# A two-layer decoder step on one Trainium2 core: who reads the page numbers and issues the page loads, how a window is loaded, and where one filler projection stands

## The chip, the core and the metric

The kernel runs on one core of one Trainium2 chip. The core has a matrix engine (TensorE; PE in the profile, with PEld for its weight loads), a vector engine (VectorE, DVE), an activation engine (ScalarE, ACT), a general engine (GpSimd, POOL) and SyncE (SP), which here only issues DMAs. The engines run their own instruction streams and meet by semaphores. The metric is the time of one execution on the device, in microseconds.

## The reference

One inference step of a decoder layer, done for two layers, on 256 prompt tokens and 8 x 4 sample tokens that share all weights. Cut to what matters here:

```
z = x @ w_in                                   # conv branch and attention branch
ua, ug, q, kc, vc, ks, vs, kw, vw, gates... = split(z)
u = ua * sigmoid(ug); conv = depthwise_conv31(u); conv_out = silu(LN(conv)) @ w_conv_out
k_cmp = compress(kc_all); v_cmp = compress(vc_all)      # 32-row blocks, stride 16: (rows+pe) @ w1, gelu, @ w2
o_cmp, p_cmp = cmp_attention(q, k_cmp, v_cmp)
idx = select_blocks(p_cmp)                              # top 16 blocks of 64 rows
o_slc = slc_attention(q_rot, ks_all, vs_all, idx)
o_win = window attention (512 rows)
attn_out = (gate-weighted sum of the three) @ w_attn_out
x = LN(alpha*x + (sig(g_A)*conv_out + sig(g_B)*attn_out) @ w_o)
x = LN(alpha*x + (silu(x@w_gate) * (x@w_up)) @ w_down)
```

For the sample tokens the past of `kc, vc` (cmp) and `ks, vs` (slc) lies in pages of 128 rows in a pool; a table of 64 numbers says which page is which. The past window lies in `state_win`.

## The kernel before, in words

**Weights.** Everything is a matrix product of 128 x 128 blocks. The weights of a layer are cut into 116 chunks of 512 KB (8 blocks). SP loads chunk j into one of three slots `wch` (`load_chunk`, L482) once POOL has finished with chunk j-3. ACT writes its rounded high part `w_hi` (`high_part`, L1057; it waits until PE is through with chunk j-3), POOL the rest `w_lo` (`low_part`, L605), and PE multiplies three times: high x high, low x high, high x low (L686 to L688). So up to three chunks are split and waiting when PE asks for one, and no new one can be split until PE has used one and ACT has come round to it.

**The order of PE's work** is written out by hand. A layer begins with the outputs o = 0 to 17 of the input projection, then `compress(0)` to `compress(3)` (L782: the page batch i against `w1`), between them `second(i)` (L795), which needs the gelu of batch i from DVE (`hg_ready`). The outputs from 18 on are filler: `fill(layer)` (L729) puts one of them (24 matmuls) wherever PE would else wait. After `compress(3)` come `second(2)`, two fills (L987, L988), `second(3)`, the convolution's statistics around one more fill, and then `group_scores(0)` (L866), the scores of sample group 0. For the jobs behind it the table `FILLS` (L99) says how many fills stand in three places of each job; for job ("g", 0) these are before `group_sum(0)`, after it, and after the next job's scores. ACT and DVE walk the same numbers (`fill_out`, ACT L1217, DVE L1777): ACT reads the filler's output, then runs `high_part` three chunks on.

**Page batches.** There are 8 batches of 16 pages (128 KB a page) in each layer: 0 to 3 of the cmp cache, for `compress(0)` to `compress(3)`, 4 to 7 of the slc cache, where `group_scores(0)` reads 4 and then 5 and `group_scores(1)` 6 and 7. They share three slots `pg` (batch i in slot i mod 3, each freed by its user, `page_user`, L443). Per page SP runs a read of the number from the table into a register (`read_numbers`, L490, line L492: `TENSOR_LOAD`, a register instruction and an assertion) and a DMA that uses it (L506). SP's order: `lead` (L522) loads chunks 0 to 20 and in chunks 2 to 17 one page each of the batches 0/1 and 2; in layer 0, where batch 0 is not there yet, that makes three pages for every chunk. `body` (L545) begins with the 16 numbers of batch 3, then chunks 21 and 22, the 16 numbers of batch 4, chunk 23, and then the DMAs of batch 3, the DMAs of batch 4, the numbers of batch 5 and its DMAs; chunk 24 comes behind them. All of this is one stream on SP, and every transfer of SP is on one queue.

**Windows.** `load_window` (L509) loads the 2 MB of one sample group as four DMAs of 512 KB: four in a row in layer 0's `lead`, and otherwise one behind every chunk or every other chunk. The state of the convolution (`load_past`, 544 KB) follows eight chunks after the next layer's first window DMA.

Of the kernel before, what the change touches and what calls it, by code (L numbers as in the profile page):

```python
# [68 lines left out]
EARLY = 18  # L69
FIRST_GU = CH_IN + CH_MIX + CH_WO  # L70
LEAD = EARLY + PAIRS
PG_SLOTS = 3

# [25 lines left out]
FILLS = {("g", 0): (1, 2, 1), ("u", 0): (0, 1, 1), ("u", 1): (0, 0, 1), ("u", 2): (0, 1, 1), ("u", 3): (0, 0, 0), ("g", 1): (1, 1, 1),  # L99
# [52 lines left out]
def decoder_kernel(nc, xT, consts, page_table, weights, small, w1, w2, cmp_pages, slc_pages, win, past_u,  # L152
                   yT, kv_out, p_conv_out, s_conv_out, win_out):
    with ExitStack() as ctx:  # L154
# [148 lines left out]
        win_in = Signal("win_in", 2, 16 * DEC_B // 2, ahead=False)  # L303
# [105 lines left out]
        carrier_pe = ctx.enter_context(nc.semaphore("carrier_pe"))  # L409
        carrier_sp = ctx.enter_context(nc.semaphore("carrier_sp"))  # L410
# [58 lines left out]
        def _(sp):  # L469
# [20 lines left out]
            def read_numbers(i, first=0, n=2 * PAGES):  # L490

                return [sp.value_load(table[0:1, bass.ds((i % 4) * 2 * PAGES + j, 1)], min_val=0, max_val=POOL - 1)  # L492
                        for j in range(first, first + n)]

            def load_pages(layer, i, first=0, n=2 * PAGES, numbers=None):

                slot = i % PG_SLOTS
                source = cmp_pages if i < 4 else slc_pages
                if numbers is None:
                    numbers = read_numbers(i, first, n)  # L500
                if first == 0:
                    user, back = before(i, 8, PG_SLOTS)
                    sig, count = page_user(user)
                    wait_alone(*sig(layer, count - back * sig.per_layer))
                for j, page in zip(range(first, first + n), numbers):
                    sp.dma_start(pg[:, slot, bass.ds(j, 1)], source[bass.ds(layer, 1), bass.ds(page, 1)].rearrange(  # L506
                        "a b p n -> p (a b) n")).then_inc(pages_in[slot].sem, 16)

            def load_window(layer, gr, rows=range(DEC_B // 2)):  # L509
                if rows[0] == 0:  # L510
                    wait_alone(*gpv_done(layer, gr))
                    wait_alone(*win_stored(layer, gr))
                for b in rows:
                    sp.dma_start(wn[:, b:b + 1], win[bass.ds(layer, 1), 4 * gr + b:4 * gr + b + 1].rearrange(
                        "a b p n -> p (a b) n")).then_inc(win_in.sem, 16)
# [6 lines left out]
            def lead(layer, first):  # L522


                for j in range(LEAD):
# [9 lines left out]
                    if EARLY - 2 * PAGES <= j < EARLY:  # L535
# [5 lines left out]
                        load_pages(layer, 2, n, 1)  # L541
# [3 lines left out]
            def body(layer, more):  # L545


                numbers = {3: read_numbers(3)}
                for j in range(LEAD, CHUNKS):
                    load_chunk(layer, j)  # L550

                    if j == EARLY + AHEAD - 2:
                        numbers[4] = read_numbers(4)
                    if j == EARLY + AHEAD - 1:
                        load_pages(layer, 3, numbers=numbers[3])
                        load_pages(layer, 4, numbers=numbers[4])
                        load_pages(layer, 5)
# [3 lines left out]
                    n = j - (EARLY + AHEAD + 5)  # L561
                    if 0 <= n < 4:
                        load_window(layer, 1, [n])
# [6 lines left out]
                    if more and 0 <= n - 2 * PAGES < 8 and n % 2 == 0:  # L570
                        load_window(layer + 1, 0, [(n - 2 * PAGES) // 2])
                    if more and n == 2 * PAGES + 8:
                        load_past(layer + 1)
# [84 lines left out]
        def _(pe):  # L658
# [271 lines left out]
            with layers(pe) as layer:  # L930
# [57 lines left out]
                fill(layer)  # L988
# [58 lines left out]
        def _(act):  # L1047
# [161 lines left out]

            for n in range(PAIRS):  # L1210
                high_part(0, n)
            hi_ready.count = 0
            with layers(act) as layer:
# [13 lines left out]
                def chunk_read(o):  # L1227

                    high_part(layer, o + PAIRS)
# [751 lines left out]
```

## Time and profile before

| | us |
|---|---|
| median of 3 runs (1072.98 to 1074.56) | 1073.44 |
| the profiled execution's own time | 1073.44 |
| its span in the trace | 1071.6 |
| PE busy | 1001.3 (93%) |
| POOL busy | 753.0 (70%) |
| DVE busy | 606.7 (57%) |
| ACT busy | 524.2 (49%) |
| mean share of the 16 DMA engines in SP's queue | 49.5% |

The span is from the first to the last recorded instruction. Busy time of an engine is the union of its instructions; register, semaphore and DMA-issuing instructions are not counted in it. A layer takes about half of the span: layer 0 is at `group_scores(0)` at 138.5 us, layer 1 at 662.7 us. In lists of waits, "idle" is the time in which the engine had nothing running just before an instruction, with the instruction or DMA that ended last before it.

### The profile page before, as it was taken

The page shows a single profiled execution, that of the slowest core. Times are in us where ns is not written, and L with a number is a line of the kernel's source. Part 1 is how long each engine was busy: PE and PEld are TensorE (multiplying, and loading weights), DVE is VectorE, ACT ScalarE, POOL GpSimd, SP SyncE. Part 2 cuts the span into 40 slices and gives each one's busy share as a digit, 9 for nine tenths or more (in the row PEclk, how much of TensorE's full clock was granted, in tenths as well). Part 3 has the DMA queues.
Part 4 walks back from the last instruction along what each step waited for, and adds up shares of the span by engine and source line. Part 5 has one row for each costly group of instructions (what it writes and reads, how often), then busy time and mean ns, then how long its engine had stood idle before and what let it go on. Part 6 is the DMA issues. An engine that isn't in the chain of part 4 may idle for free.

```text
span 1071.6 us, 23755 instructions
## 1 busy us (share of the span) xinstructions
PE 1001.3 (93%) x7646; PEld 945.2 (88%) x7646; DVE 606.7 (57%) x1386; ACT 524.2 (49%) x966; POOL 753.0 (70%) x1081
## 2 busy tenths in 40 slices
PE   4999989988999999999979999898989999999995
PEld 4998878787999999999979977787879899999995
DVE  1868765556777555511446794745575775554124
ACT  3352563454565555544354335643455566555335
POOL 5778744344778888898757785543349788889984
PEclk9999999999999999999999999999999999999998
DMA  8775687421356764555367456664115345545542
GB/s 307 226 245 200 194 275 239 173 80 60 109 166 191 225 217 160 172 172 166 100 218 230 155 178 201 237 211 157 61 60 168 128 158 161 172 160 164 174 152 87
DMA packets 78342, 185.11 MB, mean 173 GB/s; under 512 B 9474, under 2 KB 42626, under 8 KB 77698
## 3 DMA queue, kind: packets, MB, share of 16 engines
q1 hardware_dynamic: 74322, 171.22, 49.5%
q10 hardware_dynamic: 3744, 11.40, 2.8%
q8 instruction: 64, 1.05, 0.4%
q0 software_dynamic: 144, 0.89, 0.2%
q14 instruction: 68, 0.56, 0.2%
HBM read 170.90 MB, written 12.57 MB: 171 GB/s over the span
## 4 chain that ended last, share of the span: by engine, by line
POOL 67%; issue 31%; POOLq 1%; DMA 1%; ACT 0%; SPq 0%
POOL w_lo L614 61%; POOL hid L637 3%; POOL res L635 2%; POOL res L644 1%; DMA wch<-weights_in 0%; POOLq L608 0%; DMA table<-page_table_in 0%; POOLq L632 0%; POOLq L154 0%; ACT w_hi L1064 0%; POOL hid L638 0%; POOL hid L635 0%; SPq L472 0%; POOLq L620 0%; POOLq L624 0%
## 5 line engine op out<-in xcount | busy, mean ns | idle before, releaser
L614 POOL TENSOR_TENSOR w_lo<-wch,w_hi 128x256 fp32r<-128x256 f32 x940 | 685.6, 766 | 307.2 <-ACT w_hi L1064 306.8
L686 PE MATMUL proj<-x_hi,w_hi 128*128 128x290 f32 (+1 forms) x1248 | 379.5, 304 | 25.4 <-POOL w_lo L614 20.6
L687 PE MATMUL proj<-x_hi,w_lo 128*128 128x290 f32 (+1 forms) x1248 | 370.4, 297 | 0.0
L688 PE MATMUL proj<-x_lo,w_hi 128*128 128x290 f32 (+1 forms) x1248 | 369.8, 296 | 0.0
L1064 ACT ACTIVATE w_hi<-wch 128x1024 fp32r<-128x1024 f32 x235 | 247.6, 1054 | 159.2 <-PE proj L709 75.7
L686 PEld LDWEIGHTS proj<-x_hi,w_hi 128*128 128x128 f32 x1248 | 235.6, 189 | 32.3 <-issue 21.5
L687 PEld LDWEIGHTS proj<-x_hi,w_lo 128*128 128x128 f32 x1248 | 236.5, 190 | 0.5
L688 PEld LDWEIGHTS proj<-x_lo,w_hi 128*128 128x128 f32 x1248 | 236.3, 189 | 0.0
L707 PE MATMUL proj<-hid_hi,w_hi 128*128 128x288 f32 x352 | 104.3, 296 | 0.0
L709 PE MATMUL proj<-hid_lo,w_hi 128*128 128x288 f32 x352 | 103.6, 294 | 0.0
L708 PE MATMUL proj<-hid_hi,w_lo 128*128 128x288 f32 x352 | 103.3, 293 | 0.0
L1436 DVE SCALAR_TENSOR_TENSOR ps_s<-u_p,sm,ps_s 128x256 f32<-128x256 f32 x232 | 94.5, 483 | 4.2
L1520 DVE SCALAR_TENSOR_TENSOR res<-proj,res 128x288 f32<-128x288 f32 x32 | 14.6, 456 | 130.9 <-PE proj L709 109.6
L1069 ACT ACTIVATE res<-res,top 128x256 f32<-128x256 f32 (+5 forms) x108 | 46.7, 433 | 52.9 <-DVE top L1597 48.5
L1850 DVE COPY sums_of<-proj 128x2 f32<-128x2 f32 x88 | 14.0, 160 | 99.9 <-PE proj L688 99.7
L708 PEld LDWEIGHTS proj<-hid_hi,w_lo 128*128 128x128 f32 x352 | 66.2, 188 | 0.1
L707 PEld LDWEIGHTS proj<-hid_hi,w_hi 128*128 128x128 f32 x352 | 66.1, 188 | 0.1
L709 PEld LDWEIGHTS proj<-hid_lo,w_hi 128*128 128x128 f32 x352 | 66.1, 188 | 0.0
L1069 ACT ACTIVATE q_raw<-q_raw,sums_of 128x288 f32<-128x288 f32 x44 | 23.6, 538 | 76.0 <-DVE q_raw L1863 76.0
L686 PE MATMUL proj<-mix_hi,w_hi 128*128 128x288 f32 x128 | 38.6, 302 | 0.5 <-POOL w_lo L614 0.5
L770 PE MATMUL ps_t<-cst 128*128 128x128 f32 x324 | 38.7, 277 | 0.0
L770 PEld LDWEIGHTS ps_t<-cst 128*128 128x128 f32 x324 | 37.4, 192 | 1.2 <-issue 1.0
(287 smaller groups left out, 1568.4 us busy)
## 6 DMA issues: line engine op xcount, KB each, us to landing
wch<-weights_in SPq DMA_DIRECT2D x235, 512.0 KB, 3.7
pg<-cmp_pages_in SPq DMA_DIRECT2D x128, 128.0 KB, 2.9
pg<-slc_pages_in SPq DMA_DIRECT2D x128, 128.0 KB, 2.5
wn<-win_in SPq DMA_DIRECT2D x16, 512.0 KB, 5.4
win_out<-wn ACTq DMA_DIRECT2D x4, 2048.0 KB, 8.5
hid<-w_in SPq DMA_DIRECT2D x2, 1024.0 KB, 5.5
kv_out<-kv ACTq DMA_DIRECT2D x2, 864.0 KB, 3.9
res<-xT_in SPq DMA_DIRECT2D x1, 1152.0 KB, 5.4
```

What stands on the lines that cost most here:

```text
L614: last = nc.gpsimd.tensor_tensor(lo[:, cols], raw[:, cols], hi[:, cols].bitcast(F32), ALU.subtract)
L637: do(nc.gpsimd.tensor_tensor(out, out, tap_s[:], ALU.add))
L686: mm(ps, hi[:, kb], x[0][:, kb, 0:n], start=kb == 0, stop=False)
L687: mm(ps, lo[:, kb], x[0][:, kb, 0:n], start=False, stop=False)
L688: last = mm(ps, hi[:, kb], x[1][:, kb, 0:n], start=False, stop=kb == KD - 1)
L707: mm(ps, hi, hid_hi[:, kb], start=kb == 0, stop=False)
L708: mm(ps, lo, hid_hi[:, kb], start=False, stop=False)
L709: last = mm(ps, hi, hid_lo[:, kb], start=False, stop=kb == KF - 1)
L770: mm(ps_m[:, 0:P], k("mean_c"), k("cos")[:, 0:P], start=True, stop=True)
L1064: hi_ready.up(nc.scalar.activation(w_hi[:, n % PAIRS].rearrange("p k n -> p (k n)"), wch[:, n % SLOTS].rearrange("p k n -> p (k n)"), ACT. ...
L1069: i = nc.scalar.activation(out, in_, func, **kw)
L1436: i = v.scalar_tensor_tensor(out=out, in0=in_, scalar=conv_w[:, c, tap:tap + 1], in1=so_far, op0=ALU.mult, op1=ALU.add)
```

## The change

Four things are changed.

1. SP's page numbers: `read_numbers` is gone. `load_pages` reads the up to 16 numbers of a batch itself, directly before that batch's DMAs (for a whole batch: the reads, then the wait for the slot, then the DMAs). So the numbers of batches 3 and 4 are now read behind chunk 23.
2. Page batch 2 is no longer issued by SP. A new function `load_page` on ACT reads one number and issues one page's DMA behind the `high_part` of outputs 2 to 17.
3. Windows: one DMA of 2 MB for a group instead of four of 512 KB; `load_past` for the next layer now directly follows the window's DMA, where the first of the four stood.
4. One fill is taken from before `second(3)` (on PE, ACT and DVE), and the first number of `FILLS["g", 0]` goes from 1 to 2.

```diff
-FILLS = {("g", 0): (1, 2, 1), ...
+FILLS = {("g", 0): (2, 2, 1), ...
-        win_in = Signal("win_in", 2, 16 * DEC_B // 2, ahead=False)
+        win_in = Signal("win_in", 2, 16, ahead=False)
...
-            def load_pages(layer, i, first=0, n=2 * PAGES, numbers=None):
+            def load_pages(layer, i, first=0, n=2 * PAGES):
...
+                for at in range(first, first + n, READ_AHEAD):
+                    some = range(at, min(at + READ_AHEAD, first + n))
+                    pages = [sp.value_load(table[0:1, bass.ds((i % 4) * 2 * PAGES + j, 1)], min_val=0, max_val=POOL - 1) for j in some]
+                    if at == 0:
+                        user, back = before(i, 8, PG_SLOTS)
+                        sig, count = page_user(user)
+                        wait_alone(*sig(layer, count - back * sig.per_layer))
+                    for j, page in zip(some, pages):
+                        sp.dma_start(pg[:, slot, bass.ds(j, 1)], source[bass.ds(layer, 1), bass.ds(page, 1)].rearrange(
+                            "a b p n -> p (a b) n")).then_inc(pages_in[slot].sem, 16)
+
+            def load_window(layer, gr):
+                wait_alone(*gpv_done(layer, gr))
+                wait_alone(*win_stored(layer, gr))
+                win_in.up(sp.dma_start(wn[:], win[bass.ds(layer, 1), 4 * gr:4 * gr + 4].rearrange("a b p n -> p (a b) n")))
...
-                        load_pages(layer, 2, n, 1)
...
-                numbers = {3: read_numbers(3)}
                 for j in range(LEAD, CHUNKS):
                     load_chunk(layer, j)
-                    if j == EARLY + AHEAD - 2:
-                        numbers[4] = read_numbers(4)
                     if j == EARLY + AHEAD - 1:
-                        load_pages(layer, 3, numbers=numbers[3])
-                        load_pages(layer, 4, numbers=numbers[4])
-                        load_pages(layer, 5)
+                        for i in range(3, 6):
+                            load_pages(layer, i)
...
-                    n = j - (EARLY + AHEAD + 5)
-                    if 0 <= n < 4:
-                        load_window(layer, 1, [n])
+                    if j == EARLY + AHEAD + 5:
+                        load_window(layer, 1)
...
-                    if more and 0 <= n - 2 * PAGES < 8 and n % 2 == 0:
-                        load_window(layer + 1, 0, [(n - 2 * PAGES) // 2])
-                    if more and n == 2 * PAGES + 8:
+                    if more and n == 2 * PAGES:
+                        load_window(layer + 1, 0)
                         load_past(layer + 1)
...
                 second(layer, 2)
                 fill(layer)
-                fill(layer)
                 second(layer, 3)
...
+            def load_page(layer, i, j):
...
+                page = act.value_load(table[0:1, bass.ds((i % 4) * 2 * PAGES + j, 1)], min_val=0, max_val=POOL - 1)
+                act.dma_start(pg[:, slot, bass.ds(j, 1)], cmp_pages[bass.ds(layer, 1), bass.ds(page, 1)].rearrange(
+                    "a b p n -> p (a b) n")).then_inc(pages_in[slot].sem, 16)
...
                 def chunk_read(o):
                     high_part(layer, o + PAIRS)
+                    if EARLY - 2 * PAGES <= o:
+                        load_page(layer, 2, o - (EARLY - 2 * PAGES))
```

How the change moves instructions on SP, behind chunk 20 and layer 0's window, in the kernel before (the left number is the source line; 16 reads or 16 DMAs stand where the dots are):

```order
L514 DMA wn<-win_in 128x1024 x4
L576 UNCONDITIONAL_BRANCH
L492 TENSOR_LOAD table
...
L487 DMA wch<-weights_in 128x1024 x2
L492 TENSOR_LOAD table
...
L487 DMA wch<-weights_in 128x1024
L506 ISA
L506 DMA pg<-cmp_pages_in 128x256
...
L506 DMA pg<-slc_pages_in 128x256
```

The same place in the changed kernel:

```order
L510 DMA wn<-win_in 128x4x1024
L564 UNCONDITIONAL_BRANCH
L489 DMA wch<-weights_in 128x1024 x3
L498 TENSOR_LOAD table
...
L504 DMA pg<-cmp_pages_in 128x256
L498 TENSOR_LOAD table
...
L504 DMA pg<-slc_pages_in 128x256
```

Chunks 21 to 23 stand in front, and behind them the 16 reads of batch 3, its 16 DMAs, the 16 reads of batch 4, its DMAs, the 16 reads of batch 5 and its DMAs; before, the reads of batches 3 and 4 stood ahead of chunks 21 and 23.

On ACT, from the end of `second_out(2)` (the two `v_misc` rows) through the fills to `second_out(3)` (the `k_cmp` row), before:

```order
L1069 ACTIVATE v_misc<-ps_o 31x256
L1076 REGISTER_ALU
L1077 ACTIVATE hid<-proj 128x288
L1060 REGISTER_ALU
L1064 ACTIVATE w_hi<-wch 128x1024
L1076 REGISTER_ALU
L1077 ACTIVATE hid<-proj 128x288
L1064 ACTIVATE w_hi<-wch 128x1024
L1069 ACTIVATE k_cmp<-ps_o 128x128
```

The same place in the changed kernel:

```order
L1056 ACTIVATE v_misc<-ps_o 31x256
L1063 REGISTER_ALU
L1064 ACTIVATE hid<-proj 128x288
L1047 REGISTER_ALU
L1051 ACTIVATE w_hi<-wch 128x1024
L1056 ACTIVATE k_cmp<-ps_o 128x128
```

One filler's output (`hid<-proj`) and one chunk's high part (`w_hi`) are gone from here; PE's 24 matmuls of that filler are gone from the same place. They stand again behind the first window store:

```order
L1295 DMA win_out<-wn 128x4x1024
L1063 REGISTER_ALU
L1064 ACTIVATE hid<-proj 128x288
L1047 REGISTER_ALU
L1051 ACTIVATE w_hi<-wch 128x1024
L1063 REGISTER_ALU
L1064 ACTIVATE hid<-proj 128x288
L1047 REGISTER_ALU
L1051 ACTIVATE w_hi<-wch 128x1024
L1056 ACTIVATE res,hid<-res,top 128x1056
```

Before, there was one such pair between the store and the exponential of the 1056 columns.

On ACT again, between the high parts made for outputs 2 and 3 (`chunk_read`), the first page load in the changed kernel:

```order
L1051 ACTIVATE w_hi<-wch 128x1024
L1203 ISA
L1205 TENSOR_LOAD table
L1205 ISA x2
L1206 ISA
L1206 DMA pg<-cmp_pages_in 128x256
L1047 REGISTER_ALU
L1050 REGISTER_ALU
L1051 ACTIVATE w_hi<-wch 128x1024
```

Before, the two `w_hi` rows followed each other with only register instructions between them.

## Rows read from the trace of the kernel before

**Rows 1.** PE's waits, whole span: us in total, times, longest us.
```profile
PE proj L686 <- POOL w_lo L614: 21.2, 9, 15.0
PE ps_t L848 <- DVE imp L1613: 8.3, 10, 1.3
```

**Rows 2.** PE's timeline around `second(3)` of layer 0: start us, us, what.
```profile
122.26 0.40 PE L686 MATMUL proj<-x_hi,w_hi 128*128 128x288 f32 x1
...
128.62 0.29 PE L688 MATMUL proj<-x_lo,w_hi 128*128 128x288 f32 x1
129.04 0.43 PE L810 MATMUL ps_o<-res,w_sb 64*64 64x128 f32 x4
```

**Rows 3.** DVE's timeline there: the gelu of batch 3, last step, both layers.
```profile
128.21 0.68 DVE L1487 SCALAR_TENSOR_TENSOR res<-sq 64x512 f32<-64x512 f32 x1
...
652.40 0.68 DVE L1487 SCALAR_TENSOR_TENSOR res<-sq 64x512 f32<-64x512 f32 x1
```

**Rows 4.** PE's timeline, layer 1: `second(3)`, and the wait at `group_sum(0)`.
```profile
653.23 0.44 PE L810 MATMUL ps_o<-res,w_sb 64*64 64x128 f32 x4
...
671.11 0.39 PE L897 MATMUL ps_t<-imp,cst 128*128 128x14 f32 x2 [0.52 <-DVE imp L1641]
```

**Rows 5.** SP's number reads (L492) of batch 3, layer 0: ns min/median/max, first and last start.
```profile
L492 SPq TENSOR_LOAD <-table x16: 261/261/275, 81.8 to 90.0; - x16
```

**Rows 6.** SP's timeline, both layers: chunks 21 to 23, then the DMAs of batch 3.
```profile
90.54 9.88 SPq L487 DMA_DIRECT2D wch<-weights_in  x3
100.69 8.49 SPq L506 DMA_DIRECT2D pg<-cmp_pages_in  x16
...
621.06 9.23 SPq L506 DMA_DIRECT2D pg<-cmp_pages_in  x16
```

**Rows 7.** SP's DMAs (L506) of batch 5 with their landing: layer 0, then layer 1.
```profile
L506 SPq DMA_DIRECT2D pg<-slc_pages_in x16: 332/333/668, 127.4 to 136.2; - x16
DMA to landing us min/median/max: 2.1/2.5/5.6
...
L506 SPq DMA_DIRECT2D pg<-slc_pages_in x16: 332/333/487, 649.5 to 657.5; - x16
DMA to landing us min/median/max: 1.9/2.2/6.8
```

**Rows 8.** POOL's timeline: the low part of chunk 20, layer 0 and layer 1.
```profile
88.22 3.01 POOL L614 TENSOR_TENSOR w_lo<-wch,w_hi 128x256 fp32r<-128x256 f32 x4 [1.68 <-ACT w_hi L1064]
...
612.48 3.01 POOL L614 TENSOR_TENSOR w_lo<-wch,w_hi 128x256 fp32r<-128x256 f32 x4 [2.44 <-ACT w_hi L1064]
```

**Rows 9.** PEld's timeline: `group_scores(0)` comes to batch 5, layer 0 and layer 1.
```profile
140.96 0.15 PEld L885 LDWEIGHTS ps_s<-pg,qs_rot 128*32 128x32 f32 x4 [0.67 <-DMA pg<-slc_pages_in]
...
664.38 0.19 PEld L885 LDWEIGHTS ps_s<-pg,qs_rot 128*32 128x32 f32 x6 [0.31 <-issue]
```

**Rows 10.** PE's timeline: `compress(3)` begins, layer 0 and layer 1.
```profile
114.40 6.90 PE L792 MATMUL ps_w<-pg,hid 128*128 128x256 f32 x31
...
638.65 6.68 PE L792 MATMUL ps_w<-pg,hid 128*128 128x256 f32 x30
```

**Rows 11.** PE's timeline at the start of the kernel.
```profile
14.97 0.60 PE L686 MATMUL proj<-x_hi,w_hi 128*128 128x288 f32 x1 [14.97 <-POOL w_lo L614]
...
18.25 0.66 PE L691 MATMUL ps_t<-x_hi,w_hi 128*128 128x288 f32 x2
18.73 0.32 PE L686 MATMUL proj<-x_hi,w_hi 128*128 128x288 f32 x1
...
19.16 0.43 PE L691 MATMUL ps_t<-x_hi,w_hi 128*128 128x288 f32 x2
```

**Rows 12.** Busy us (count) of PE, PEld, DVE, ACT, POOL, PEclk, DMA share, GB/s.
```profile
28.00:64.00 36.00, 36.00 (x272) 35.00 (x270) 24.02 (x61) 13.78 (x21) 26.65 (x38) 1.00 0.74 231
138.00:144.00 6.00, 5.52 (x38) 2.15 (x39) 4.68 (x12) 0.60 (x2) 1.46 (x3) 1.00 0.95 292
265.00:270.00 5.00, 4.04 (x25) 3.48 (x26) 1.92 (x5) 1.19 (x3) 2.78 (x4) 0.79 0.21 57
1060.00:1064.00 4.00, 0.04 (x1) 0.00 (x0) 3.13 (x7) 3.65 (x9) 0.00 (x0) 0.90 0.00 0
```

**Rows 13.** SP's timeline in layer 0's lead: three pages and a chunk.
```profile
36.73 1.94 SPq L506 DMA_DIRECT2D pg<-cmp_pages_in  x3
38.72 0.43 SPq L487 DMA_DIRECT2D wch<-weights_in  x1
```

**Rows 14.** PE's waits from 28 to 80 us, then from 535 to 560 us.
```profile
PE ps_w L778 <- POOL w_lo L614: 0.7, 1, 0.7
PE proj L686 <- POOL w_lo L614: 0.5, 1, 0.5
...
PE proj L686 <- DVE u_s L1701: 2.2, 1, 2.2
PE proj L686 <- POOL w_lo L614: 2.1, 2, 1.4
```

**Rows 15.** ACT waiting for a weight chunk beside the window loads, 350 to 400 us.
```profile
ACT w_hi L1064 <- DMA wch<-weights_in: 3.5, 8, 1.1
```

More of the change, by code:

```diff
@@ L72 @@
 PG_SLOTS = 3
+READ_AHEAD = 16
 SMALL = {}
@@ L96 @@
 JOBS = [("g", 0)] + [("u", n) for n in range(4)] + [("g", 1)] + [("u", n) for n in range(4, 8)]
-FILLS = {("g", 0): (1, 2, 1), ("u", 0): (0, 1, 1), ("u", 1): (0, 0, 1), ("u", 2): (0, 1, 1), ("u", 3): (0, 0, 0), ("g", 1): (1, 1, 1),
+FILLS = {("g", 0): (2, 2, 1), ("u", 0): (0, 1, 1), ("u", 1): (0, 0, 1), ("u", 2): (0, 1, 1), ("u", 3): (0, 0, 0), ("g", 1): (1, 1, 1),
          ("u", 4): (0, 1, 2), ("u", 5): (0, 0, 2), ("u", 6): (0, 2, 1), ("u", 7): (0, 1, 0)}
@@ L409, in decoder_kernel @@
         carrier_pe = ctx.enter_context(nc.semaphore("carrier_pe"))
+        carrier_act = ctx.enter_context(nc.semaphore("carrier_act"))
         carrier_sp = ctx.enter_context(nc.semaphore("carrier_sp"))
@@ L488, in load_chunk @@
                     "a p (k n) -> p (a k) n", k=8)))
-            def read_numbers(i, first=0, n=2 * PAGES):
-                return [sp.value_load(table[0:1, bass.ds((i % 4) * 2 * PAGES + j, 1)], min_val=0, max_val=POOL - 1)
-                        for j in range(first, first + n)]
-            def load_pages(layer, i, first=0, n=2 * PAGES, numbers=None):
+            def load_pages(layer, i, first=0, n=2 * PAGES):
                 slot = i % PG_SLOTS
                 source = cmp_pages if i < 4 else slc_pages
[L499 to L515, printed above, removed]
+                for at in range(first, first + n, READ_AHEAD):
[8 more added lines that the diff above has]
+                            "a b p n -> p (a b) n")).then_inc(pages_in[slot].sem, 16)
@@ L1207, in group_act @@
                     do(sq[:, 0:1024], ps_s[:].rearrange("p a n -> p (a n)"), ACT.Copy, gpt_act)
+            def load_page(layer, i, j):
+                slot = i % PG_SLOTS
+                if j == 0:
+                    user, back = before(i, 8, PG_SLOTS)
+                    sig, count = page_user(user)
+                    act.wait_ge(*sig(layer, count - back * sig.per_layer))
+                    act.sem_inc(carrier_act, 1)
+                page = act.value_load(table[0:1, bass.ds((i % 4) * 2 * PAGES + j, 1)], min_val=0, max_val=POOL - 1)
+                act.dma_start(pg[:, slot, bass.ds(j, 1)], cmp_pages[bass.ds(layer, 1), bass.ds(page, 1)].rearrange(
+                    "a b p n -> p (a b) n")).then_inc(pages_in[slot].sem, 16)
             for n in range(PAIRS):
@@ L1212, in _ @@
             hi_ready.count = 0
+            act.wait_ge(table_in, 16)
             with layers(act) as layer:
@@ L1275, in _ @@
                 second_out(layer, 2)
-                fill_out()
                 fill_out()
```

1 line of the change is left out of this document (removed).

## The prediction

> **What bounds the kernel now.** I read the engines' busy shares first: PE is busy for 1001.3 of 1071.6 us. The list of PE's waits comes next [rows 1]: the largest group is 21.2 us for POOL's low parts, of which 15.0 are the start of the kernel, and the next is 8.3 us in ten small gaps. So PE's instruction stream is the clock of this kernel: whatever puts a hole into it lengthens the span by that hole, and taking work off another engine gives back at most a gap that PE has now. Then I went along PE's timeline and looked, at each place that the change touches, at what comes just in time. Two things do: the gelu for `second(3)`, and page batch 5 for `group_scores(0)`. The change moves both edges the wrong way.
>
> The sum is made against the profiled execution: 1071.6 us of span and 1.8 us around it, 1073.44 us, which is also the median.
>
> **The moved fill.** Two fills stand between `second(2)` and `second(3)`. They start at 122.26 and the last matmul starts at 128.62, that is 3.3 us for a fill, and `second(3)` starts at 129.04 [rows 2]. DVE finishes the gelu it needs at 128.21 + 0.68 = 128.89 [rows 3]. That chain starts with `compress(3)` and runs on DVE and ACT; no fill is in it. With one fill less PE is there at about 125.7 and still starts `second(3)` at 129.04: a hole of 3.3 us, and the 24 matmuls are done later. Layer 1 is the same (gelu at 653.08, `second(3)` at 653.23) [rows 3, 4]. What the fill can cover in its new place is the gap before `group_sum(0)`, 0.5 us in layer 1 and none in layer 0 [rows 4]. Cost: 3.3 + 2.8 = 6.1 us. Bounds: 0 if the gelu came 3.3 us earlier, which nothing in the change does, and about 5 a layer if chunk 23, whose high part moves behind the window store on ACT, also came late. I take it as covered by the next wait.
>
> **The page numbers.** The 16 reads of a batch start from 81.8 to 90.0 and the next DMA is at 90.54 [rows 5, 6]: 8.7 us of SP for 16 numbers, 0.54 each. Before, 16 reads were done while SP had nothing to issue (chunk 21 had to wait anyway), and 16 more ahead of chunk 23. Now SP takes chunk 23 as soon as POOL has finished chunk 20, at 88.22 + 3.01 = 91.2 in layer 0 [rows 8]. Then: chunk 23 until 91.7, the reads of batch 3 until 100.4, its first DMA at 100.7. That is where it was (100.69) [rows 6]. But between the DMAs of batches 3 and 4 there are now 16 reads, so batches 4 and 5 and chunk 24 go 8.7 us later. The last DMA of batch 5 goes from 136.2 to 144.9, and with the median landing of 2.5 us it is in at 147.4 [rows 7]. PE takes batch 5 at 140.96, after a wait of 0.67 us for just this DMA [rows 9]; in the changed kernel it arrives at the same time (the hole above is before it) and waits until 147.4: +6.4 us. In layer 1 SP ran ahead before: batch 3 started at 621.06. Now chunk 23 waits for POOL until 615.5 [rows 8], batch 3 starts at 616.0 + 8.7 + 0.3 = 625.0, 3.9 us later; with the second group of reads, batch 5's last DMA goes from 657.5 to 670.1 and lands at 672.3, where PE wants it at 664.5 [rows 7, 9]: +7.8 us. Batch 3 stays in time: its last DMA goes at about 109 and 634, and `compress(3)` starts at 114.40 and 638.65 [rows 6, 10]. Bounds for one layer: 0, if these reads overlap DMA issue in some way that the single stream of SP does not show, and 9.5 at the slowest landing seen, 5.6 [rows 7]. That one fell beside the store of the convolution's state, which will be over by then, so I take the median.
>
> The Trainium skill, "DMA: Bandwidth & Descriptors", section "Latency and other measured facts", gives a floor of about 600 ns for such a register load. By it 16 reads would take an estimated 9.6 us, and each page term would be 0.9 us larger. This trace has 0.26 us for the load alone and 0.54 for one number with all that goes with it, and the sum goes by that.
>
> Chunk 24 is issued 8 to 9 us later as well. Its high part is made behind the window store, after 150 us, so it has time.
>
> **TensorE's clock.** PE will now stand still for about 6.5 us before batch 5. The rows show what that does: at the end the last matmul is over at 1060.04, and in 1060 to 1064 the granted clock is 0.90 [rows 12], so it falls to the lower level (1.2 GHz) at about 1063.2, 3.2 us after the last work. At the start a pair of matmuls takes 0.66 us until 18.73 and 0.43 after [rows 11]: 3.8 us at half speed, 1.9 us lost. I charge 1.9 us for each of the two long waits, 3.8 us. The wait of 3.3 us before `second(3)` may cost the same, but what it slows ends before batch 5 is there. Bounds: 0, and 3.8 a layer if two falls count.
>
> **Batch 2 on ACT.** In layer 0's lead SP takes 1.94 us for the DMAs of three pages, 0.43 for the chunk [rows 13] and 1.3 for the reads left out of that row, 3.7 us for a chunk that PE uses up in 3.2. SP is never idle there, while the DMA engines are busy for 0.74 [rows 12]. Afterwards PE has waits of 0.7 and 0.5 us for low parts [rows 14]. With a third of the pages gone SP keeps up: -1.2 us. The Trainium skill, "DMA: Bandwidth & Descriptors", section "Issuing engines are not separate DMA queues", says that issuing on several engines saves only the sequencer's time. If that saving were small here, as it says is usual, this term would be nothing; the rows say that the sequencer is what is short. In layer 1 PE waits 2.2 us for DVE, which waits for the small weights' DMA, and then up to 1.4 for a low part whose chunk was late [rows 14]. Before these DMAs SP has one page less to issue, 1.1 us, and then another: -1.6 us. Bounds for both: 0 and -4.7. ACT pays 1.1 us for a page. It works for less than 14 us of the 36 from 28 to 64 [rows 12], and the last page is issued before DVE takes up the compressed rows, so I put nothing on it; if it were all exposed it would be 1 us a layer.
>
> **Windows.** The merged window with the convolution's state is 2.5 MB ahead of a chunk, at the 292 GB/s that the rows show [rows 12] 9 us, so the chunk lands some 4 us later than now. ACT already waits for chunks there, 3.5 us in eight waits [rows 15], while PE has no gap, since three chunks are split ahead of it. I take 0; bounds 0 and +4, once.
>
> **Sum.** 6.1 + 6.4 + 7.8 + 3.8 - 1.2 - 1.6 = +21.3 us, which gives 1094.7. I say 1094.
>
> **The rivals.**
> - *The numbers cost less than their 8.7 us on the path.* If batch 5 were in time, what is left is the fill less the lead's gain, +6.1 - 2.8 = +3.3: 1076.7. For it: SP ran 4 us ahead in layer 1. Against it: in layer 0 PE waits for this very DMA already [rows 9]. A half-way case, +4 a layer without the clock, gives 1085.
> - *Everything adds.* Chunk 23 late by 2 us a layer, the clock twice in each layer, the window's burst: +21.3 + 4 + 3.8 + 2 = 1104.
> - *About no change.* Batch 5 in time and the hole before `second(3)` filled by half: 1074 to 1075.
> - *Faster.* The mechanism is the lead: SP is relieved by a third, both starts of the layers lose their gaps, at most 1.2 + 3.5 us, and the fill ends in a place that needs it. That is 1069 to 1071. It decides only if batch 5 lands before 141 and 664.5 us and the gelu is there by 125.7; I find no row for either.
>
> **How the numbers follow.** The full mechanism 0.62 (own range 1088 to 1101), numbers cheaper 0.17, everything adds 0.10, no change 0.07, faster 0.04. The range 1081 to 1102 holds the first case, about half of the second and some of the third. A measurement tells about 0.2%, 2.1 us, from no change; so faster 0.04, same 0.07, slower 0.89.
>
> **What would show it.** A wait of PE at the batch-5 scores for the page DMA, 6 to 8 us in each layer; a wait of about 3.3 us before `second(3)` for DVE's gelu; granted clock under 1 in the microseconds behind the batch-5 wait; SP's DMAs of batch 5 ending near 145 and 670; the two small waits near 68 and 76 us gone. The prediction is wrong if PE's wait at batch 5 is under 3 us, or if `compress(3)` waits for batch 3.

## The result, and the profile after

| | before | after |
|---|---|---|
| median | 1074.00 us (1072.98 to 1074.79, 4 runs) | 1106.86 us (1102.54 to 1110.21, 4 runs) |
| span of the profiled run | 1071.6 us | 1105.7 us |
| mean granted clock | 0.994 | 0.977 |

The ratio is 1.0304, with a 95% interval from 1.0262 to 1.0348: the changed kernel is 28 to 37 us slower. The prediction was 1094, range 1081 to 1102. The direction was right, the size was not: 21.3 us of extra span were forecast, and the profiled run has 34.1. One execution of the kernel `r_busy` below fell into a slow state (1261.9 us at a granted clock of 0.755) and is not in its ratio.

The list of PE's waits in the changed kernel (us in total, times, longest us) answers to [rows 1]:

```profile
PE proj L674 <- POOL w_lo L602: 24.3, 8, 14.9
PE ps_s L873 <- DMA pg<-slc_pages_in: 13.5, 2, 7.4
PE ps_o L798 <- DVE res L1488: 8.4, 4, 3.3
PE ps_t L836 <- DVE imp L1614: 7.7, 10, 1.3
```

Two groups are new: 13.5 us for the pages of batch 5, and 8.4 us for the gelu, which was 1.9 before. The low parts' group has grown by 3.1. The next lines are PE's timeline at these places, both layers (start us, us, what, idle time before and what ended it); they answer to [rows 2, 4, 9]:

```profile
127.54 0.44 PE L798 MATMUL ps_o<-res,w_sb 64*64 64x128 f32 x4 [3.28 <-DVE res L1488]
148.84 1.07 PE L873 MATMUL ps_s<-pg,qs_rot 128*32 128x512 f32 x2 [7.45 <-DMA pg<-slc_pages_in]
389.50 0.61 PE L674 MATMUL proj<-x_hi,w_hi 128*128 128x290 f32 x1 [3.22 <-POOL w_lo L602]
672.64 0.69 PE L798 MATMUL ps_o<-res,w_sb 64*64 64x128 f32 x4 [3.27 <-DVE res L1488]
```

The two holes of 3.3 us before `second(3)` are where the prediction put them, and so is the page wait. The hole at 389.50, in the FFN of layer 0, was not predicted. SP's DMAs of batch 5 in both layers, with their landing, answer to [rows 7]:

```profile
L504 SPq DMA_DIRECT2D pg<-slc_pages_in x16: 332/333/345, 136.8 to 144.6; - x16
...
DMA to landing us min/median/max: 2.1/2.4/4.2
```

```profile
L504 SPq DMA_DIRECT2D pg<-slc_pages_in x16: 332/333/333, 681.6 to 689.5; - x16
...
DMA to landing us min/median/max: 2.0/2.3/4.1
```

The last issue at 144.6 was predicted as 144.9. But PE starts at 148.84, which is 4.2 us behind it: the slowest landing, not the median. Layer 1 is the same, 689.5 + 4.1 = 693.6, and PE's weight load is at 693.68. The windows over these places (columns as in [rows 12]) show the clock:

```profile
128.00:132.00 4.00, 4.00 (x16) 2.97 (x15) 1.00 (x11) 1.49 (x4) 3.01 (x4) 0.62 0.34 104
...
144.00:148.00 4.00, 0.00 (x0) 0.00 (x0) 1.31 (x7) 1.72 (x3) 0.00 (x0) 0.75 0.79 242
148.00:152.00 4.00, 3.16 (x12) 0.87 (x14) 0.00 (x0) 0.00 (x0) 0.00 (x0) 0.50 0.81 234
...
388.00:392.00 4.00, 2.50 (x10) 2.50 (x11) 2.12 (x5) 3.00 (x5) 4.00 (x7) 0.54 0.38 116
392.00:396.00 4.00, 4.00 (x21) 4.00 (x20) 0.42 (x2) 0.00 (x0) 2.95 (x5) 0.60 0.45 149
```

Behind each of these holes the granted clock falls, so that windows of 4 us show 0.50 to 0.62: TensorE is at its lower level (1.2 GHz) for some microseconds, behind the short holes too.

The lag of an instruction is how much later it starts than the same instruction in the trace of before. Its growth gives the bill by stages. "Measured" is the growth in the stage, "predicted" are the prediction's own terms:

| stage | lag at its end | measured | predicted |
|---|---|---|---|
| layer 0 up to its FFN | +13.7 | 13.7 | 10.4 (6.4 page, 3.3 fill, 1.9 clock, -1.2 lead) |
| layer 0's FFN and output | +19.5 | 5.8 | 0 |
| layer 1's lead | +19.4 | -0.1 | -1.6 |
| rest of layer 1 | +34.1 | 14.7 | 12.5 (7.8 page, 2.8 fill, 1.9 clock) |

### The profile page after: what moved, and what is told of

It is laid out like the page before. It is cut to its first block, busy times and chain, and to the rows that moved or that the text cites. A ratio compares the mean times of both kernels' runs of the same rounds, so it can differ in the third digit from the quotient of the medians.

```text
span 1105.7 us, 23747 instructions
## 1 busy us (share of the span) xinstructions
PE 1017.0 (92%) x7646; PEld 955.9 (86%) x7646; DVE 604.8 (55%) x1386; ACT 523.7 (47%) x966; POOL 749.3 (68%) x1081
## 4 chain that ended last, share of the span: by engine, by line
POOL 65%; issue 33%; POOLq 1%; DMA 1%; ACT 0%; SPq 0%
POOL w_lo L602 59%; POOL hid L625 3%; POOL res L623 2%; POOL res L632 0%; DMA wch<-weights_in 0%; DMA table<-page_table_in 0%; POOLq L596 0%; POOLq L620 0%; POOLq L155 0%; ACT w_hi L1051 0%; POOL hid L626 0%; POOL hid L623 0%; SPq L474 0%; POOLq L608 0%; POOLq L612 0%
```

## The experiments

All are compared with the kernel before, run beside them on the same chip; a cost in us is the ratio less 1, times 1074.

### The four parts, each alone

**Windows and state** (`w_only`): only part 3 of the change.

```diff
-                    if more and 0 <= n - 2 * PAGES < 8 and n % 2 == 0:
-                        load_window(layer + 1, 0, [(n - 2 * PAGES) // 2])
-                    if more and n == 2 * PAGES + 8:
+                    if more and n == 2 * PAGES:
+                        load_window(layer + 1, 0)
                         load_past(layer + 1)
```

> The kernel before with one part of the change: each window is one transfer of 2 MB, and the convolution's state follows it directly. Theory (the burst holds up the weight chunk behind it): in the changed kernel the chunk behind the 2.5 MB lands 9.1 us after its issue, PE waits 3.2 us for a low part in layer 0's FFN and then runs some 5 us at half clock, 5.8 us later in all. Alone it should cost about the same: +4 to +6.5 us, a PE wait of about 3 us near 375 us into the span. Rival (the prediction's own term: three split chunks cover the late one, and the loss in the changed kernel came from its other parts): within +-1 us, and no PE wait over 1 us there.

Measured: ratio 1.0077 (1.0060 to 1.0093), +8.3 us. The theory's place and its PE wait were right, its size a bit low; the prediction's zero is refuted. The chunk behind the window is issued at 363.27, ACT gets it at 372.58, and PE then stands still:

```profile
372.58 1.06 ACT L1059 ACTIVATE w_hi<-wch 128x1024 fp32r<-128x1024 f32 x1 [5.79 <-DMA wch<-weights_in]
```

```profile
376.55 0.61 PE L681 MATMUL proj<-x_hi,w_hi 128*128 128x290 f32 x1 [3.29 <-POOL w_lo L609]
```

**Reads** (`r_only`): only part 1.

```diff
-                numbers = {3: read_numbers(3)}
...
-                    if j == EARLY + AHEAD - 2:
-                        numbers[4] = read_numbers(4)
...
-                        load_pages(layer, 3, numbers=numbers[3])
-                        load_pages(layer, 4, numbers=numbers[4])
+                        load_pages(layer, 3)
+                        load_pages(layer, 4)
```

> The kernel before with one part of the change: the page numbers of batches 3 and 4 are read behind chunk 23, directly before their DMAs. Theory (SP's reads set batch 5's arrival, the slowest landing counts, and TensorE's clock falls behind each long wait): PE waits of 7 to 8 us in layer 0 and 6 to 8 us in layer 1 before the batch-5 scores, 1.7 to 2.5 us of slow clock behind each: +17 to +20 us. Rival 1 (the reads cost as predicted with the median landing): +14.2 and 3.8 of clock, about +18, but then the holes are 6.4 and 7.8. Rival 2 (in the changed kernel the page wait is made by the batch-2 pages or the window on the queue, and the reads are cheap): under +5 us.

Measured: ratio 1.0198 (1.0181 to 1.0215), +21.3 us. The waits, each PE's first matmul on batch 5:

```profile
148.65 1.07 PE L882 MATMUL ps_s<-pg,qs_rot 128*32 128x512 f32 x2 [8.77 <-DMA pg<-slc_pages_in]
...
682.62 1.07 PE L882 MATMUL ps_s<-pg,qs_rot 128*32 128x512 f32 x2 [8.59 <-DMA pg<-slc_pages_in]
```

The reads alone make the page waits; batch 2 on ACT, the window and the fill are not needed for them. Both holes are 0.6 to 0.8 us longer than the theory had.

**Fill** (`f_only`): only part 4.

```diff
-FILLS = {("g", 0): (1, 2, 1), ...
+FILLS = {("g", 0): (2, 2, 1), ...
...
                 fill(layer)
-                fill(layer)
                 second(layer, 3)
```

> The kernel before with one part of the change: one fill moves from before second(3) to before group_sum(0). Theory (each layer gets a hole of 3.3 us, and the clock falls behind it too): 2 x 3.3 us of holes and 1.7 to 2.8 us of slow clock behind each, less the 0.7 us wait for batch 5 in layer 0 and the 0.5 us gap at group_sum(0) in layer 1: +9 to +11 us, a granted clock under 1 in the 8 us behind the holes. Rival (the prediction's term: the hole alone): +5.5 to +6.1 us and no fall of the clock. Second rival (the fill covers something in its new place): under +3 us.

Measured: ratio 1.0124 (1.0108 to 1.0141), +13.3 us, more than either theory. PE's timeline shows what both had left out:

```profile
153.44 0.40 PE L686 MATMUL proj<-x_hi,w_hi 128*128 128x288 f32 x1 [2.17 <-ACT hid L1076]
...
158.32 0.40 PE L686 MATMUL proj<-x_hi,w_hi 128*128 128x288 f32 x1 [1.41 <-POOL w_lo L614]
```

In its new place the fill finds two more fills behind it, whose output buffers and weight chunks depend on ACT, and ACT is behind the window store: 3.6 us a layer, in place of some 1 us of shorter waits that the kernel before has here. In the changed kernel neither wait exists at this place (PE's timeline has no wait for `hid` there), because batch 5 comes so late that ACT is done. It was a bound of the prediction ("about 5 a layer if chunk 23 ... also came late. I take it as covered by the next wait"), and it was covered.

**Batch 2 on ACT** (`a_only`): only part 2.

> The kernel before with one part of the change: batch 2's 16 page numbers are read and its DMAs issued by ACT instead of SP. Theory from the two traces: the lead of layer 0 loses its gaps near 68 and 76 us (-1.2 to -1.5 us), layer 1's start gains nothing, because the small weights and the low part behind them stay late: -1.0 to -1.6 us. Rival (the prediction's term): -2.8 us, half of it in layer 1. Second rival (ACT pays the 1.1 us a page on the path): 0 to +2 us.

Measured: ratio 0.9998 (0.9988 to 1.0008), -0.2 us, with 10 runs. The -2.8 us of the prediction are refuted, and the theory's -1.0 to -1.6 isn't reached either. In the trace, which is of the fastest of the ten, the first layer's `compress(0)` is 1.3 us earlier and layer 1's start adds 0.5; in the changed kernel's trace it adds 0.1.

### What the window's burst is made of

**Window merged, state late** (`w_late_past`):

```diff
                     if more and n == 2 * PAGES:
                         load_window(layer + 1, 0)
+                    if more and n == 2 * PAGES + 8:
                         load_past(layer + 1)
```

> The kernel before with each window as one transfer of 2 MB, but the convolution's state left eight chunks behind it, as before. With the state directly behind the window it was 7.7 us slower, the chunk behind landed after 9.2 us, and PE waited 3.3 us and then lost 2.5 at half clock. Theory (bytes ahead of the chunk decide: 0.54 MB less at some 290 GB/s is 1.9 us earlier): the chunk lands after some 7.3 us, PE waits about 1.4 us near 375 us, the clock stays up or nearly, +1 to +3.5 us. Rival (the merge alone does it, whatever the state does): +6 to +8 us.

Measured: ratio 1.0032 (1.0020 to 1.0045), +3.4 us, within the theory's range, though landing and wait are each 0.9 us longer than it had. The chunk behind lands after 8.2 us (its group's slowest), and PE waits:

```profile
374.48 0.40 PE L682 MATMUL proj<-x_hi,w_hi 128*128 128x290 f32 x1 [2.29 <-POOL w_lo L610]
```

```profile
376.00:380.00 4.00, 4.00 (x32) 4.00 (x31) 1.58 (x4) 0.75 (x2) 4.00 (x6) 1.00 0.67 232
```

The clock stays at 1.00 behind this hole of 2.3 us, where in `w_only` it was 0.50 in 376 to 380 behind one of 3.3. So the state costs one further microsecond of hole, and in these traces the clock with it.

These kernels give the rule that the prediction lacked. Chunk j is issued when POOL frees its slot; PE then still has three chunks of 3.2 us to work on, some 10 us in the changed kernel (376.30 to 386.3). In that time the chunk must land, ACT must take 1.06 us and POOL 3.01. So a landing of up to about 5.9 us is free, and every further microsecond is PE's hole: 9.1 gives 3.2 (measured 3.22), 9.2 gives 3.3 (3.29), 8.2 gives 2.3 (2.29), and in `wa` below 9.3 gives 3.4 (3.41). Before, the slowest chunk there landed in 5.6 us: the four pieces left 0.3 us of margin.

```profile
L487 SPq DMA_DIRECT2D wch<-weights_in x10: 327/328/328, 358.9 to 388.4; - x10
...
DMA to landing us min/median/max: 3.6/4.3/5.6
```

### What the reads cost, and the clock behind the wait

**Only batch 4's numbers late** (`r4_only`); those of batch 3 stay where they are:

```diff
-                    if j == EARLY + AHEAD - 2:
-                        numbers[4] = read_numbers(4)
...
-                        load_pages(layer, 4, numbers=numbers[4])
+                        load_pages(layer, 4)
```

> The kernel before with only the numbers of batch 4 read late (between the DMAs of batch 3 and 4); those of batch 3 stay ahead of chunk 21. Moving both groups cost 20.8 us. Theory (SP stands free from about 81 us until POOL is done with chunk 20 at 91; that slack holds one group of 16 reads, so only the second group that leaves the front lands on the path): within +-1.5 us of before, DMAs of batch 5 ending at 136 to 137 and before 661 us. Rival (each group costs its half): +8 to +12 us.

Measured: ratio 1.0059 (1.0042 to 1.0076), +6.3 us. Both expectations missed: one group is neither free nor half of the 21.3. SP's timeline:

```profile
89.36 1.28 SPq L487 DMA_DIRECT2D wch<-weights_in  x3
93.44 8.56 SPq L506 DMA_DIRECT2D pg<-cmp_pages_in  x16
111.41 27.73 SPq L506 DMA_DIRECT2D pg<-slc_pages_in  x32
```

Chunk 23 is out at about 90.6, but the DMAs of batch 3 start only at 93.44, 7.3 us earlier than before [rows 6] and not 8.7: between them SP issues nothing for 2.8 us. (Their slot is freed by `compress(0)`, which has just ended then; that this is the cause is read from the code and was not tried.) Batch 4 starts 2.0 us later than before, the last DMA of batch 5 about 2.6 later, and PE waits 3.24 us in layer 0 and 3.03 in layer 1. There were some 7 us of free time on SP for these reads, and the first group overdraws them by 2. The second group doesn't add all of its 8.7. These are SP's DMAs of batches 4 and 5 in `r_only` and before:

```profile
116.70 27.99 SPq L506 DMA_DIRECT2D pg<-slc_pages_in  x32
```

```profile
109.42 27.10 SPq L506 DMA_DIRECT2D pg<-slc_pages_in  x32
```

They end at 144.7 in `r_only`, 139.1 in `r4_only` and 136.5 before. So in layer 0 the second group adds 5.6 us: that fits 8.7 less the 2.8 us in which SP stood still here.

**Extra matmuls in the page wait** (`r_busy`, `r_busy2`). Both are `r_only` with a number of matmuls of 128 columns in front of batch 5, whose results are overwritten by the next fill; 34 in the first, 46 in the second:

```diff
                 for b in range(4):
+                    if gr == 0 and b == 2:
+                        hold_clock(layer, 46)
                     if b % 2 == 0:
```

> The kernel with only the reads moved (20.8 us slower than before) and 34 extra matmuls of 128 columns, whose results nobody reads, in the two waits of 8.8 and 8.6 us before the batch-5 scores. Theory: the waits themselves are 8.8 - 0.7 + 8.6 = 16.7 us and the clock behind them is the rest, about 4: +15.5 to +17.5 us, clock 1.00 behind the wait. Rival (the rest is not the clock but late chunks behind the reads): +20 to +21 us as without them.

> The kernel with only the reads moved (21.3 us slower than before) and 46 extra matmuls of 128 columns, whose results nobody reads, in the page wait of 8.8 us, so that no idle time is left in it. Theory (1.5 to 2.5 us a layer of the cost is slow clock behind the wait): clock 1.00 behind it and, with up to 1 us a layer by which the extra matmuls run over, +17 to +19.5 us. Rival (the clock behind the wait costs nothing on the path): +21 to +23 us.

Measured: 1.0177 (1.0139 to 1.0214) and 1.0183 (1.0165 to 1.0202), +19.0 and +19.7 us. Neither is told apart from the 1.0198 of `r_only`, and neither decides between its theory and its rival. With 34 there was still a hole of 1.9 us, and the clock fell behind it; in layer 1 the hole was 1.7 us and the clock stayed at 1.00. These are windows of `r_busy` in layer 0:

```profile
148.00:152.00 4.00, 2.07 (x20) 1.68 (x22) 0.00 (x0) 0.00 (x0) 0.00 (x0) 0.99 0.70 236
152.00:156.00 4.00, 4.00 (x17) 0.81 (x9) 0.00 (x0) 0.00 (x0) 0.00 (x0) 0.58 0.82 235
```

With 46 it stayed up in both layers (windows of `r_busy2`, then of `r_only`):

```profile
148.00:152.00 4.00, 3.98 (x37) 3.59 (x40) 0.00 (x0) 0.00 (x0) 0.00 (x0) 1.00 0.76 229
```

```profile
144.00:148.00 4.00, 0.00 (x0) 0.00 (x0) 1.30 (x7) 0.23 (x2) 0.00 (x0) 0.58 0.79 233
148.00:152.00 4.00, 3.35 (x14) 0.97 (x16) 0.00 (x0) 0.00 (x0) 0.00 (x0) 0.56 0.80 232
```

The extra matmuls ran over, so that the first scores of batch 5 came 2.8 us later than in `r_only` (3.4 in layer 1), of which 1.1 (1.6) were there before the page wait. But the next common point was only 1.4 us later (282.56 against 281.10), and 1.1 in layer 1 (811.26 against 810.14). What they gave back is 1.4 and 2.3 us. That is one trace of each kernel, and it agrees with the prediction's 1.9 for each page wait; by the times alone it stays open.

### The clock behind the hole of 3.3 us

**Extra matmuls before `second(3)`** (`f_busy`): `f_only` with 13 of them behind the one fill.

> The kernel before with the fill moved (13.8 us slower alone) and 13 extra matmuls of 128 columns before second(3), whose results nobody reads, in the hole of 3.3 us. Theory (the hole is 3.3, the fill's late output costs 2.2 + 1.4 in its new place, and 1 to 2 us a layer are the clock behind the hole): clock 1.00 in 128 to 136 us and +9.5 to +12 us. Rival (the clock fall is hidden under what follows, as the prediction had it): +13 to +14 us as without them.

Measured: ratio 1.0067 (1.0050 to 1.0084), +7.2 us, against +13.3 without them, and the intervals don't touch. The gelu still sets the start of `second(3)`; the only difference is that PE isn't idle ahead of it. The windows, `f_only` first:

```profile
128.00:132.00 4.00, 3.31 (x16) 2.80 (x17) 2.10 (x17) 2.65 (x6) 2.19 (x3) 0.50 0.59 162
132.00:136.00 4.00, 4.00 (x18) 3.29 (x18) 1.42 (x2) 0.84 (x2) 0.80 (x2) 0.68 0.98 247
```

```profile
128.00:132.00 4.00, 3.60 (x33) 3.21 (x33) 3.56 (x21) 3.62 (x9) 0.59 (x1) 1.00 0.33 97
132.00:136.00 4.00, 4.00 (x28) 3.74 (x27) 1.42 (x2) 1.64 (x3) 2.44 (x4) 1.00 0.98 253
```

So a hole of 3.3 us costs about as much again, 3 us a layer, behind it. That was more than the theory's 1 to 2. The traces have less in layer 1: between the hole and the window store the lag against `f_only` shrinks by 2.8 us in layer 0 and by 1.7 in layer 1. There the clock falls later, behind the wait of 2.16 us for the fill's late output (`f_busy`):

```profile
684.00:688.00 4.00, 4.00 (x21) 3.86 (x20) 3.53 (x7) 3.57 (x6) 4.00 (x5) 0.62 0.93 370
```

**The changed kernel with both** (`after_busy`): 13 before `second(3)` and 26 before batch 5.

> The changed kernel with 13 extra matmuls of 128 columns before second(3) and 26 before the batch-5 scores, whose results nobody reads, in the time in which TensorE stands still (3.3 and 6 to 7.5 us): the waits stay as long, only the engine isn't idle in them. Theory (a part of the loss is TensorE at its lower clock behind the holes, some 8 to 10 us in all, more than the 3.8 of the prediction): 7 to 10 us faster than the changed kernel, +23 to +26 us against before, clock near 1 behind both holes. Rival (the prediction's 3.8 us): +28 to +30 us. Second rival (the extra matmuls delay more than they hold): +33 or more.

Measured: ratio 1.0265 (1.0237 to 1.0294), +28.5 us: the rival's 28 to 30 and not the theory's 23 to 26. It is 4.2 below the changed kernel's 32.7, but with overlapping intervals. PE still waits for the pages, and it waits for them up to about the same time as without the extra matmuls:

```profile
149.39 1.07 PE L881 MATMUL ps_s<-pg,qs_rot 128*32 128x512 f32 x2 [4.65 <-DMA pg<-slc_pages_in]
```

It was 148.84 in the changed kernel and is 149.39 here. The first hole's clock costs up to 3 us where nothing waits behind it, but here it is hidden by the page wait, as the prediction had it.

### Do the parts add up?

Alone they cost 8.3, 21.3, 13.3 and -0.2, in sum 42.7; together 32.7. Seven kernels look for the 10 us: the changed kernel without one part, and pairs on top of before.

> The changed kernel with the page numbers read as before (batch 3 ahead of chunk 21, batch 4 ahead of chunk 23): windows, fill and batch 2 on ACT stay changed. The parts alone cost 7.7 (windows), 20.8 (reads), 13.8 (fill) and -0.3 us (batch 2 on ACT), 42 in sum, while together they cost 33. Theory (the fill's late output on ACT and POOL, 3.6 us a layer, lies under the wait for batch 5, so reads and fill overlap and nothing else does): the parts without the reads add up, +19 to +22 us, so the reads are worth only 11 to 14 in the changed kernel. Rival (windows and the others overlap instead): under +15 us.

> The changed kernel with the fill back before second(3): windows, reads and batch 2 on ACT stay changed. Theory (overlap of fill and reads): windows 7.7 + reads 20.8 - 0.3 = +27 to +29 us, so the moved fill is worth only 4 to 6 us here against 13.8 alone. Rival (the overlap is elsewhere): 33 - 13.8 = +18 to +20 us.

> The changed kernel with the windows in four pieces and the convolution's state late, as before: reads, fill and batch 2 on ACT stay changed. Theory (the windows are independent of the rest): 33 - 6 to 7.7 = +25 to +27 us, no PE wait near 390 us. Rival (without the burst something else is late there, since the fill and reads overlap accounts for all of the 9 us that the parts exceed the whole): +29 or more.

> The kernel before with the reads and the fill moved, and nothing else. Alone they cost 21.3 and 13.3 us. Theory (the fill's late output on ACT and POOL, 2.2 + 1.4 us a layer, lies under the wait for batch 5, and half of the clock's fall behind the first hole too): +26 to +29 us. Rival (they add up): +33 to +36 us.

> The kernel before with the windows merged and the reads moved. Alone they cost 8.3 and 21.3 us. Theory (different places, no overlap): +28 to +31 us. Rival (the merged window changes what SP has to do ahead of the reads and takes back part of the loss, as the changed kernel without the moved fill, +21.4 us, suggested): +20 to +24 us.

> The kernel before with the windows merged and the fill moved. Alone they cost 8.3 and 13.3 us. Theory (no overlap): +20 to +23 us. Rival (as the changed kernel with the reads as before, +13.5 us, suggested): +13 to +16 us.

> The kernel before with the windows merged and batch 2 on ACT. Alone they cost 8.3 and -0.2 us. Theory (batch 2 on ACT gains only where something else has made SP late, and with merged windows it does: 5 to 7 us): +1.5 to +4 us. Rival (the two add up and the rest is scatter between chips): +7 to +9 us.

| kernel | parts | ratio (95%) | us | sum of its parts |
|---|---|---|---|---|
| `rf` | reads, fill | 1.0265 (1.0247 to 1.0284) | 28.5 | 34.6 |
| `wr` | windows, reads | 1.0265 (1.0242 to 1.0287) | 28.5 | 29.6 |
| `wf` | windows, fill | 1.0183 (1.0162 to 1.0204) | 19.7 | 21.6 |
| `wa` | windows, ACT | 1.0036 (1.0023 to 1.0049) | 3.9 | 8.1 |
| `no_window` | reads, fill, ACT | 1.0252 (1.0221 to 1.0282) | 27.1 | 34.4 |
| `no_reads` | windows, fill, ACT | 1.0126 (1.0090 to 1.0162) | 13.5 | 21.4 |
| `no_fill` | windows, reads, ACT | 1.0199 (1.0170 to 1.0227) | 21.4 | 29.4 |
| changed kernel | all | 1.0304 (1.0262 to 1.0348) | 32.7 | 42.7 |

The theories of `rf`, `wr`, `wa` and, within the interval, `no_window` and `wf` were met; those of `no_reads` and `no_fill` were missed by 5.5 us or more, towards their rivals. Reads and fill overlap by about 6 us. Under the page wait lie both the fill's late output (no wait for `hid` or a low part is left there in the trace of `rf`) and the slow clock behind the first hole; how the 6 us split between the two was not measured. Windows add up with either within the intervals. The rest lies with batch 2 on ACT, which is worth nothing alone and about 4 us beside merged windows (`wa` against `w_only`; their intervals don't touch), more in `no_reads` and `no_fill` with wider intervals. I don't know why. In the trace of `wa` PE still waits 3.41 us near 374 us and the clock falls behind it, so the burst itself isn't mended. The traces don't show the gain: with batch 2 on ACT the span of the profiled execution is 1.2 us shorter in `wa` than in `w_only`, 0.2 shorter in `no_reads` than in `wf`, and 0.4 longer in `no_fill` than in `wr`. These pairs ran on different chips, each beside its own kernel before, so a difference between chips isn't excluded. This part stays open.

### A version that beats both

**Batch 2 on ACT, and layer 1's small weights a chunk earlier** (`a_small`):

```diff
-                    if j == SLOTS:
+                    if j == (SLOTS if first else SLOTS - 1):
                         small_in.up(sp.dma_start(w1_sb, ...
```

> A version meant to beat both kernels: the kernel before with batch 2 on ACT, and in layer 1 the two small weights of compress issued one chunk earlier (behind chunk 2 instead of chunk 3), since DVE waits 9.5 us for them there and PE 2.2 us for DVE. If PE's wait at 559 us is set by them: 1 to 2 us faster than before. Rival (the weight chunks behind come later by their bytes and PE waits for a low part instead): no difference, within +-1 us.

Measured: ratio 0.9954 (0.9936 to 0.9973), median 1070.57 us beside 1073.64: 3 to 7 us faster than before, where the theory had 1 to 2. In the trace of before PE waits here three times: for a low part, for DVE, which waited 9.5 us for these weights, and for a low part again. In the new one the first wait has grown, the second has shrunk and the third is gone (before, then `a_small`):

```profile
546.86 0.41 PE L686 MATMUL proj<-x_hi,w_hi 128*128 128x288 f32 x1 [0.66 <-POOL w_lo L614]
...
552.57 0.40 PE L686 MATMUL proj<-x_hi,w_hi 128*128 128x288 f32 x1 [2.24 <-DVE u_s L1701]
...
557.43 0.40 PE L686 MATMUL proj<-x_hi,w_hi 128*128 128x288 f32 x1 [1.39 <-POOL w_lo L614]
```

```profile
547.45 0.40 PE L686 MATMUL proj<-x_hi,w_hi 128*128 128x288 f32 x1 [1.51 <-ACT sig_u L1077]
...
552.37 0.40 PE L686 MATMUL proj<-x_hi,w_hi 128*128 128x288 f32 x1 [1.45 <-POOL w_lo L614]
```

The two lines of `a_small` are at the places of the first two lines of before (62 and 86 matmuls behind the layer's first). Together the waits shrink by 1.3 us, from 4.3 to 3.0, and the spans differ by 2.3. The times say more than the trace explains. Nor was the small weights' move tried alone: against `a_only` (-0.2 us) the intervals don't touch, but the trace of `a_only` has the third wait gone too, and there the second is 1.90.

## Why the prediction was off

- **The failed step is the windows.** "ACT already waits for chunks there ... while PE has no gap, since three chunks are split ahead of it. I take 0; bounds 0 and +4, once." It predicted the late chunk well (some 4 us later; 9.1 against 5.6 at most before). It didn't subtract that from a cover: 10 us, less 4.1 of ACT and POOL, leave 5.9 for the landing. The hole is 3.2 us. With the clock behind it the stage costs 5.8 in the trace of the changed kernel and 6.0 in that of `w_only`, whose times say 8.3. This one term is nearly half of the miss of 12.8 us of span, and it is outside its own bound of +4. With 5.8 in its place the sum would be 1100.5.
- **The page wait: right mechanism, short by 1.5 to 2 us a layer.** SP's times were met within 0.3 us (144.6 for 144.9) in layer 0; in layer 1 the last issue, 689.5 less the lag of 19.4, is the 670.1 of the prediction. The median landing was the wrong row: PE needs all 16 pages, and the last came after 4.2 and 4.1 us. The upper bound in the prediction used the slowest one. (The rest of layer 1's excess is within this.) One reading behind it was wrong and did no harm: chunk 21 did not "have to wait anyway". SP issues it at 90.54 before, and at 81.11 in `r_only`, where the reads aren't in front of it.
- **The hole before `second(3)`: right, 3.28 and 3.27 for 3.3.** That its clock would be hidden under the page wait was right as well (`after_busy`), and so was that the fill's late output would be.
- **The clock behind the page waits: 1.9 each was about right** (1.4 and 2.3 from the traces of `r_busy2`), but two falls were left out. One is behind the burst's hole. The other is near 280 us, where the granted clock is 0.50 in 280 to 284 and the changed kernel loses 1.3 us against the one before, whose own fall, near 270, is shorter.
- **The lead: -2.8 was wrong, -0.2 measured alone.** In layer 0 the gaps near 68 and 76 us did go, and the lag shrinks by 1.9 us there in the changed kernel's trace; in layer 1 only 0.1 came. The times of `a_only` (-1.3 to +0.9 us) hardly show it, and why stays open.
- **Of the rivals,** "everything adds" (1104, chance 0.10) is nearest to 1106.9. It had the clock twice and the window at 2 us, but chunk 23 late by 2 us a layer, which did not happen in the changed kernel. "Numbers cheaper", "no change" and "faster" are refuted by the waits above.

## What to carry over

When a step puts more bytes ahead of something on the same queue, don't ask whether a buffer is "ahead": write down the time from its issue to its use, take off every engine that must still touch it, and compare what is left with the slowest landing (here 10.0 - 1.06 - 3.01 = 5.9 us, of which 5.6 were used before). Waits for a batch end with its slowest transfer. And price a hole of PE in a stream that is otherwise full with the clock behind it, unless a longer wait follows, which hides the clock's part. The moved work itself is still to be done.

## What the runs showed of the hardware

- Behind PE's holes of 3.2 to 3.3 us the granted clock fell, to 0.50 to 0.62 in windows of 4 us, at a loss of 1.7 to 3 us. Behind shorter ones it fell in some and not in others: not behind 2.3 (`w_late_past`) and 1.7 us (`r_busy`, layer 1), but behind 1.9 (`r_busy`, layer 0) and 2.2 (`f_busy`, layer 1). So the length of the hole alone doesn't decide.
- A DMA of 512 KB on the same queue took 3.6 to 5.6 us to land where the window came in pieces of 512 KB, 8.2 behind 2 MB (`w_late_past`), and 9.1 to 9.3 behind 2.5 MB (the changed kernel, `w_only`, `wa`).
- Issuing 32 page DMAs from ACT cost nothing that could be measured (-0.2 us, -1.3 to +0.9), though each came with its own read of a number; in the changed kernel their median landing was 4.2 us, where SP's cmp pages, other batches, were at 2.9.
- The first matmul, which waits for the first weights, started between 13.85 and 16.43 us in the traces, whatever the kernel. So two single traces may differ by 2 us for nothing, and differences are better taken from a common point behind the start.
